# The row loads and sums of the second block's first gate, moved from one output projection to the gated unit and the branch projections after it

## What is computed

```
mod = silu(c) @ w_mod + b_mod                 # 6 x 2048 values, second block
sh1, sc1, g1, sh2, sc2, g2 = split(mod, 6)
...
x = rms_norm(x, final_g)                      # end of the first block
h = rms_norm(x, norm1_g) * (1 + sc1) + sh1
q, k, v, u, gates = split(h @ w_in)           # attention, state-space branch, 2 branch gates
y_ssm = y * sigmoid(y @ w_glu + b_glu)        # the gated unit
merged = sigmoid(gate_a) * (y_attn @ w_attn_br) + sigmoid(gate_s) * (y_ssm @ w_ssm_br)
x = x + g1 * (merged @ w_out)                 # g1 is first needed here
```

## Time and profile before

| | |
|---|---|
| time of 3 launches | median 3036.22 us, 3032.48 to 3045.45 |
| the profiled execution itself | 3027.13 us, of it 3025.4 us span (first to last instruction) |
| mean granted TensorE clock | 0.98 |
| PE busy | 2879.7 us, 95% of the span |
| POOL busy | 1828.3 us, 60% |
| DVE busy | 1689.8 us, 56% |
| ACT busy | 1455.1 us, 48% |
| DMA | 620.46 MB, 205 GB/s on average |

### The profile page before, as it was taken

How to read it: one execution, slowest core, us unless ns; L and a number is a source line. 1 busy time by engine, 2 the same in 40 slices (tenths; PEclk the granted TensorE clock), 3 DMA queues, 4 the chain that set the end, 5 groups by cost and what they waited for, 6 DMA issues and landing times.

```text
span 3025.4 us, 49352 instructions
## 1 busy us (share of the span) xinstructions
PE 2879.7 (95%) x18353; PEld 2486.3 (82%) x18353; DVE 1689.8 (56%) x2879; ACT 1455.1 (48%) x2231; POOL 1828.3 (60%) x756
## 2 busy tenths in 40 slices
PE   7799999999889989999997999999999999999999
PEld 5688886777768888878877888899987888888888
DVE  2477972899533668247669999673324444442000
ACT  3222223556422432248645777675445555555443
POOL 1244443333233565445575677677887888888998
PEclk9999999999999999999998999999999999999999
DMA  9877322555676695233593444444555666765665
GB/s 397 320 264 274 137 97 97 184 193 202 256 271 244 249 396 230 97 105 112 183 348 130 151 154 152 147 147 159 186 191 173 239 238 223 245 215 193 206 208 187
DMA packets 148917, 620.46 MB, mean 205 GB/s; under 512 B 16512, under 2 KB 17840, under 8 KB 129840
## 3 DMA queue, kind: packets, MB, share of 16 engines
q1 hardware_dynamic: 147632, 613.44, 57.0%
q10 hardware_dynamic: 1152, 5.24, 0.5%
HBM read 616.49 MB, written 2.12 MB: 204 GB/s over the span
## 4 chain that ended last, share of the span: by engine, by line
issue 46%; POOL 29%; PE 23%; POOLq 1%; DVE 0%; DVEq 0%
POOL w_low L690 29%; PE bank L725 16%; PE bank L726 8%; POOLq L685 0%; POOLq L689 0%; POOLq L690 0%; DVE region L1866 0%; DVE region L1869 0%; DVEq L1866 0%; POOLq L2675 0%
## 5 line engine op out<-in xcount | busy, mean ns | idle before, releaser
L690 POOL TENSOR_TENSOR w_low<-raw,w_high 128x1024 fp32r<-128x1024 f32 x752 | 1828.1, 2448 | 1186.5 <-ACT w_high L1224 1182.6
L1224 ACT ACTIVATE w_high<-raw 128x1024 fp32r<-128x1024 f32 x752 | 792.9, 1057 | 836.6 <-PE bank L738 410.2
L736 PE MATMUL bank<-h,w_high 128*128 128x256 f32 (+1 forms) x2816 | 951.8, 338 | 18.4 <-POOL w_low L690 15.2
L738 PE MATMUL bank<-h,w_low 128*128 128x256 f32 (+1 forms) x2816 | 935.6, 332 | 0.0
L737 PE MATMUL bank<-h,w_high 128*128 128x256 f32 (+1 forms) x2816 | 935.6, 332 | 0.0
L736 PEld LDWEIGHTS bank<-h,w_high 128*128 128x128 f32 x2816 | 537.7, 191 | 98.9 <-issue 28.6
L725 PE MATMUL bank<-h,w_high 128*128 128x512 f32 x1664 | 584.9, 397 | 9.6 <-POOL w_low L690 4.8
L738 PEld LDWEIGHTS bank<-h,w_low 128*128 128x128 f32 x2816 | 537.4, 191 | 51.0
L737 PEld LDWEIGHTS bank<-h,w_high 128*128 128x128 f32 x2816 | 538.0, 191 | 49.8 <-issue 0.7
L726 PE MATMUL bank<-h,w_low 128*128 128x256 f32 x1664 | 464.3, 279 | 0.0
L725 PEld LDWEIGHTS bank<-h,w_high 128*128 128x128 f32 x1664 | 314.9, 189 | 85.3 <-POOL w_low L690 6.1
(11 more groups left out here) (258 smaller groups left out, 3484.9 us busy)
## 6 DMA issues: line engine op xcount, KB each, us to landing
raw<-in_w_in SPq DMA_DIRECT2D x344, 512.0 KB, 3.7
raw<-in_w_up SPq DMA_DIRECT2D x176, 512.0 KB, 3.8
region<-in_w_rows SPq DMA_DIRECT2D x55, 1024.0 KB, 7.7
raw<-in_w_out SPq DMA_DIRECT2D x96, 512.0 KB, 6.0
raw<-in_w_down SPq DMA_DIRECT2D x96, 512.0 KB, 3.6
region<-in_w_mods SPq DMA_DIRECT2D x44, 1024.0 KB, 7.9
row_extra<-in_w_half_rows SPq DMA_DIRECT2D x86, 512.0 KB, 4.4
row_extra<-in_w_rows SPq DMA_DIRECT2D x41, 1024.0 KB, 7.6
```

Of the source, the lines that this page charges most:

```text
L690: nc.gpsimd.tensor_tensor(WL[s][:, part], RAW[s][:, part], WH[s][:, part], ALU.subtract) \
L736: nc.tensor.matmul(bank[:, 0:n], WH[slot][:, w], h, start=first and j == 0, stop=False)
L738: end = nc.tensor.matmul(bank[:, 0:n], WL[slot][:, w], h, start=False, stop=last and j == len(blocks) - 1)
L1224: return nc.scalar.activation(out, in_, func, **kw)
```

## The change

The stage "out1" becomes a stage "mid". The row loads keep their number and content. Two of the three buffers change: instead of two places of region2 they are `MODW[:, 0]` and `MODW[:, 1]`, which overlap the normalised input of `w_in2`; so row load 1 waits until `w_in2` has been multiplied (`2 * U_GLU`). SP issues them ahead of the units of `w_abr` (row loads 0 to 3 ahead of unit 0, then 4, 5, 6, 7 and 8, 9, 10, 11) and of the first three of `w_sbr` (12 and 13, 14 and 15, 16 and 17). DVE sums 0 to 3 behind the last attention head, ahead of the gated unit's products; then, behind every second tile of `w_abr`: 4, 5, 6, 7 and 8, 9, 10, 11, 12 and 13; and behind tiles 1, 3, 5 and 7 of `w_sbr`: 14, 15, 16, 17. DVE's loop over the tiles of `w_abr` and SP's loops over `w_out1`, `w_abr` and `w_sbr` are written out or become generic accordingly.

```
-    ROW_OUT1 = [ROW_EXTRA[:], *r2(0, 4096)]
+    ROW_MID = [ROW_EXTRA[:], MODW[:, 0, :], MODW[:, 1, :]]
+    mid_rows = lambda r: 4 + 5 * r // 4
...
-        def row_out1(e):
-
+        def row_mid(e):
+
+            if e == 1:
+                sp.wait_ge(halves_done, 2 * U_GLU)
...
-            if name == "w_out1":
-                two(0)
-                two(1)
-                row_out1(0)
-                sp.wait_ge(sem("at_y"), 12)
-                row_out1(1)
-                row_out1(2)
-                for t in range(4, 16):
-                    for e in range(t - 1, t + 3 if t == 15 else t):
-                        row_out1(e)
+            if name in ("w_abr", "w_sbr"):
+                first = [mid_rows(t) for t in range(8)] if name == "w_abr" else [min(18, 14 + 2 * t) for t in range(8)]
+                asked = 0 if name == "w_abr" else mid_rows(7)
+                for t in range(8):
+                    for e in range(asked, first[t]):
+                        row_mid(e)
+                    asked = first[t]
                     one(t)
                 return
...
-            else:
-                for e in range(3):
-                    rows_out1(e)
...
-                elif n < 15:
-                    rows_out1(3 + n)
...
         attended_low(7)
+        for e in range(4):
+            rows_mid(e)
...
-        with dve.Fori(0, 4) as i:
-            for s in range(4):
-                n = 4 * i + s
-                dve.wait_ge(halves_done, 2 * U_ABR + n + 1)
-                mul(tile(GATE_A, n), L[s][:, 0:T], tile(GATE_A, n)).then_inc(bank_free[s], 1)
+        for n in range(KT):
+            dve.wait_ge(halves_done, 2 * U_ABR + n + 1)
+            mul(GATE_A[:, n, :], L[n % 4][:, 0:T], GATE_A[:, n, :]).then_inc(bank_free[n % 4], 1)
+            for e in range(mid_rows(n // 2), mid_rows(n // 2 + 1)) if n % 2 else ():
+                rows_mid(e)
...
             if n >= 4:
                 merged_low(n - 4)
+            if n % 2 and n < 8:
+                rows_mid(14 + n // 2)
```

More of the change, by code:

```diff
@@ L341, in build @@
     ROW_IN1 = [ROW_EXTRA[:], *r2(4096, 6144)]
-    ROW_OUT1 = [ROW_EXTRA[:], *r2(0, 4096)]
+    ROW_MID = [ROW_EXTRA[:], MODW[:, 0, :], MODW[:, 1, :]]
     ROW_UP = [ROW_EXTRA[:]]
-    ROW_STAGES = {"in0": (ROW_IN0, 34), "att0": (ROW_ATT0, 64), "out0": (ROW_OUT0, 34), "in1": (ROW_IN1, 33), "out1": (ROW_OUT1, 18), "up": (ROW_UP, 18)}
+    ROW_STAGES = {"in0": (ROW_IN0, 34), "att0": (ROW_ATT0, 64), "out0": (ROW_OUT0, 34), "in1": (ROW_IN1, 33), "mid": (ROW_MID, 18), "up": (ROW_UP, 18)}
     ROW_FIRST, ROW_LANDED = {}, {}
@@ L537, in row_in1 @@
                 row_load("in1", e, dram["w_rows"][32 + e - 1])
-        def row_out1(e):
+        def row_mid(e):
+            if e == 1:
+                sp.wait_ge(halves_done, 2 * U_GLU)
             if e % 9 == 0:
-                row_cond("out1", e, slice(2, 3), e // 9)
+                row_cond("mid", e, slice(2, 3), e // 9)
             else:
-                row_load("out1", e, dram["w_rows"][64 + 8 * (e // 9) + e % 9 - 1])
+                row_load("mid", e, dram["w_rows"][64 + 8 * (e // 9) + e % 9 - 1])
         def row_up(e):
@@ L2068, in rows_in1, with rows_mid @@
                 row_bias(ROW_ALL["in1"], 96, 32, 2, 3).then_inc(sem("row_out"), 1)
-        def rows_out1(e):
+        def rows_mid(e):
             half, unit = e // 9, e % 9 - 1
             if unit < 0:
-                row_vector("out1", e, 5, HALF)
+                row_vector("mid", e, 5, HALF)
                 return
-            place = row_landed("out1", e)
+            place = row_landed("mid", e)
             for r in range(2):
@@ L2082, in rows_out1 @@
             if e == 17:
-                row_bias(ROW_ALL["out1"], 128, 16, 2, 3, 0).then_inc(sem("row_out"), 1)
+                row_bias(ROW_ALL["mid"], 128, 16, 2, 3, 0).then_inc(sem("row_out"), 1)
         def rows_up(e):
```

## The result

In 20 runs of each the kernel after took 3052.55 us in the median (3038.94 to 3068.03), the kernel before 3039.11 (3027.3 to 3050.65). The ratio is 1.0047, with a 95% interval of 1.0031 to 1.0063: 14 us more, between 9 and 19. The forecast was 8.3 us more and 3044.5. So the sign and the class (within 0.5%) came out, and the cost was put too low.

What follows compares the result with a forecast made beforehand. PE was taken to bound the kernel, busy for 95% of the span. A gain of 7.2 us and a cost of 15.5 gave +8.3 on the 3036.2 us median, so 3044.5 us, range 3029 to 3056.

Steps and rivals of the forecast that it cites:

- the tail: End of the last output projection: the last residual no longer waits for DVE's bias, a gain of 0.6 us.
- The stall of 3.7 us and the slow clock of 2.9: Last output projection, unit 15: PE's wait for POOL's `w_low` and the half clock behind it both go, gaining 3.7 and 2.9.
- my upper bound: Last output projection: at most 7.5 + 2.9 + 0.6 = 11 us gained, if row loads cause every idle spell there.
- The chain behind a sum: Both branches, tiles numbered 0 to 31: 13.8 us from a tile's end to the tile hanging on it, 10.65 from row-load issue.
- the 8.0 us of tile 18: State-space branch, tiles 18 and 19: row load 15 waits for 12, summed behind tile 15; 13.8 against 5.76, stall 8.0 us.
- tile 20 to be covered by the slow clock: State-space branch: the 2.2 us stall there is hidden while PE runs slowly, so only the clock's 2.9 us counts.
- I charge that once: State-space branch: slow clock costs 2.9 us, counted only behind the 8.0 us stall ahead of tile 18.
- hidden: Gated unit: DVE's some 8 us for row loads 0 to 3 cost nothing, as DVE has 0.42 us of work in 23.
- delay DVE but by themselves not PE: Both branches: a tile's bank is wanted again only 11.5 us later, so DVE's row sums alone do not stall PE.
- The full queue: Rival, both branches: three chains each 3.3 us longer behind other transfers, time 3060, halfway 3052; chance 0.16.
- The deeper cover: Rival, both branches: no chain from a row load's wait reaches PE, so the time is 3029.0; chance 0.08.
- the lost gain: Rival, last output projection: another wait replaces the one at unit 15, only the cost is left, 3051.7; chance 0.06.

Runs made afterwards that it cites:

- the reordered kernel before: Kernel before, with the output projection's last three row loads issued behind the weights of unit 15; ratio 0.9996, and 0.9983 on another chip.
- the repeat: The kernel after, unchanged, run again for a second profile; ratio 1.0074 to the kernel before.
- weights first: Kernel after, with each unit's weights issued ahead of the row loads that stood before them; ratio 1.0029 to the kernel before.
- four buffers: Kernel after, with a fourth row-load buffer, so a row load waits for the sum four before instead of three; ratio 1.002 to the kernel before.
- the bank: Kernel after, with DVE's product, sum and low half in the state-space branch working in the tile's PSUM bank; ratio 1.0046 to the kernel before.
- the sums alone: Kernel after without row loads 3 to 17; DVE still makes all 18 sums from what lies in the buffers; ratio 1.0002 to the kernel before.
- loads alone: Kernel after with all 18 row loads but no sums; a row load waits for the landing of the one three before; ratio 1.0031 to the kernel before.
- the kernel without rows: Kernel after with all 18 row loads and their sums left out; ratio 0.9984 to the kernel before.
- all three: Kernel after with a fourth row-load buffer, weights issued ahead of row loads, and DVE's state-space operations in the PSUM bank; ratio 0.9991 to the kernel before.

## Why the prediction was right or wrong

**What came out, and by what luck.** The median lies inside the range of 3029 to 3056, near its upper end. The 24.2 us of the profiled stages on top of 3036.2 would be 3060, outside it. Of the terms of the cost, 12.6 us of stalls were found as 12.1 with errors that cancel; the stalls at tiles 4 and 28 and most of the slow clock stood in no term.

**The gain: two terms right, the tail wrong.** The stall of 3.7 us and the slow clock of 2.9 behind it went: 99.6 to 93.0 us is just their sum, 6.6. For the tail I counted 0.6, and DVE's last residual did move up. PE's last product, DVE's last residual and PE's next product after stand at

```profile
1583.52 0.28 PE L726 MATMUL bank<-h,w_low 128*128 128x256 f32 x1
```
```profile
1583.84 0.48 DVE L1866 SCALAR_TENSOR_TENSOR region<-bank,mod_sb,region 128x256 f32<-128x256 f32 x1 [3.16 <-PE bank L726]
```
```profile
1587.18 1.86 PE L816 MATMUL bank<-region,const_sb 128*128 128x512 f32 x2 [3.38 <-DVE region L1801]
```

The residual follows 0.3 us behind the product instead of the 1.0 of the earlier trace rows, but PE's next product comes 3.7 us behind the last in both kernels. So the tail gave nothing, and up to the next weights 5.9 us were won of 7.2. Of the 7.5 us idle in my upper bound 2.6 lie behind the last product and belong to no stall of the projection. I had also written off DVE's 43 us, as lying beside products. With the stall taken away by a new order alone they lie on the path, as the two runs of the reordered kernel before show: the gain needs the sums to leave as well.

**The chain behind a sum: right for tiles 8, 18 and 20, too short for tile 16.** I had 13.8 us from the end of a tile to the tile that hangs on it. Tile 15's last product starts at 2144.20, and tile 18 starts at 2157.53: 13.3. SP and ACT of the kernel after on that chain, and then on the one of tile 20:

```profile
2147.25 0.33 SPq L509 DMA_DIRECT2D row_extra<-in_w_rows  x1
2147.62 0.91 SPq L464 DMA_DIRECT2D raw<-in_w_sbr  x2
2149.53 10.87 SPq L509 DMA_DIRECT2D mod_weights<-in_w_rows  x2
```
```profile
2153.99 1.06 ACT L1224 ACTIVATE w_high<-raw 128x1024 fp32r<-128x1024 f32 x1 [7.96 <-DMA raw<-in_w_sbr]
...
2166.40 1.06 ACT L1224 ACTIVATE w_high<-raw 128x1024 fp32r<-128x1024 f32 x1 [10.10 <-DMA raw<-in_w_sbr]
```

From row load 15 at 2147.25 to tile 18 are 10.3 us, where I took 10.65 from a single instance. The second of the two row loads in the third line is row load 17: it goes out as that entry ends, 2160.4, and ACT has the weights behind it 6 us later. By the fit that the Trainium skill gives for DMAs issued by GpSimd (DMA: Bandwidth & Descriptors, Anatomy of one DMA) I had estimated 5.6 us for the transfers, which SP issues here; from 2147.25 to 2153.99 it is 6.7, nearer the rows' 7.1.

For tile 16 SP and ACT read

```profile
2135.55 0.91 SPq L464 DMA_DIRECT2D raw<-in_w_sbr  x2
```
```profile
2143.68 1.06 ACT L1224 ACTIVATE w_high<-raw 128x1024 fp32r<-128x1024 f32 x1 [6.49 <-DMA raw<-in_w_sbr]
```

Row load 13 goes out right ahead, at 2135.17, and tile 16 starts at 2147.24: 12.1 us instead of 10.65, in the repeat 11.5. The queue, which I had taken as drained, wasn't: row load 12 had gone out at 2129.09, and the DMA was busy for 0.92 to 1.00 of its time from 2133 to 2143.

**The sum over the chains: wrong in two ways that partly cancel.** First, I counted the 8.0 us of tile 18 from an end of tile 15 that nothing follows, and 2.3 for tile 16 on top, though tile 16's stall lies inside that chain. By the same working it should have been 2.3 and 5.7, and then tile 20, at 21.7 against 11.5 + 5.7, would have had 4.5 and not 2.2. Measured from the end of tile 15 to the start of tile 18: 13.3 instead of 5.8, so 7.6 lost for both tiles with the clock's 1.7 among them, against my 10.3 without it. Second, I held tile 20 to be covered by the slow clock. It wasn't: its chain hangs on the start of tile 16, and 21.7 us were forecast for it, 22.7 measured. Its stall of 4.93 us is the largest of this profile; in the repeat, where tile 18 had lost 5.51, it was 0.92. At tile 8 I had 2.3 and it was 0.36; tile 4 had lost 4.1 already. All stalls of tiles 8 to 20 together come to 12.1 us against my 12.6: this term was right as a sum and wrong in its parts.

**The clock: the step that failed most, "I charge that once".** I tied it to the longest stall, 8.0 us. There was no stall of 8, but five of 2.41 to 4.93, each followed by a stretch near 1.2 GHz: some 10 us instead of 2.9. The 3.7 us of the earlier trace rows were the only case that I had read, and I took it for typical of long stalls instead of asking what the short ones (2.3) would do. The trace of before has others: in the 3 us behind the idle spells of 5.23 us (up to 1644.02) and 6.83 us (up to 1101.64) the granted clock was 0.50, behind 1.51 and 2.20 us (up to 1140.52 and 1905.58) 1.00.

**Tile 4: not seen.** I called row loads 0 to 3 hidden in the gated unit because DVE was idle there. But the DMA went from 0.47 to 0.90 of its time, ACT waited for weights (1.37 us at 2092.93), so its work on the gated unit came later, and everything behind it. DVE and ACT of the kernel after:

```profile
2094.85 6.19 DVE L1795 TENSOR_TENSOR region<-region 128x512 f32<-128x512 f32 x4 [6.88 <-ACT region L1224]
```
```profile
2099.87 1.84 ACT L1224 ACTIVATE y_ssm_high<-region 128x512 fp32r<-128x512 f32 x3 [2.18 <-DVE region L1795]
2101.61 1.99 ACT L1224 ACTIVATE w_high<-raw 128x1024 fp32r<-128x1024 f32 x2
```

The copy of tile 4's weights starts at 2101.61, 33.1 us after the first product of the gated unit; before it was 29.6 after it, with some 1.5 us to spare at the end of POOL's subtraction. Of the 3.5 us, 2.0 are the later start of DVE's four products (26.3 us after the first product of the gated unit, 24.3 before) and 1.5 their length, 6.19 us instead of 4.72. 2.41 us of stall and 1.7 of clock followed. The kernels with the weights first have no stall there, those with four buffers alone or the bank alone have 1.7 and 1.4. So the place of a row load in the queue matters here too. Neither the sums alone nor the loads alone make the stall. With the loads alone the four products take 5.94 us but start at 24.3 as before, and the copy comes 30.8 after the first product, inside the 1.5 us to spare; row load 3, which otherwise waits for the first row sum, goes out without that wait there.

**DVE's durations: taken as fixed.** That the sums "delay DVE but by themselves not PE" holds for the middle, as the run with the sums alone shows; behind it PE waited 4.10 us for DVE in that run, and most of DVE's sums of two tiles were longer than I took them for. With the stalls it doesn't hold in the middle either. From tile 20 on POOL catches up, and DVE after reads

```profile
2180.12 2.19 DVE L1801 TENSOR_TENSOR region<-region 128x256 f32<-128x256 f32 x1
2182.24 2.62 DVE L1798 TENSOR_TENSOR merged<-region,merged 128x256 fp32r<-128x256 f32 x1
2184.78 1.21 DVE L1996 SCALAR_TENSOR_TENSOR mod_weights<-mod_weights,bank 128x1024 f32<-128x1024 f32 x1
```

with row sums in between, until PE waits 4.74 us for a bank at tile 28: with the clock 7 us that no step of mine had. One operation held up in the same way (2.52 us at 2155.24) stands ahead of the sum of row load 14, and so is also in the chain of tile 20.

**The rivals.** The full queue, whose halfway price of 3052 is nearest to the median, has a share, but a small one: its mark was to be chains longer than 10.65, and only that of tile 16 was clearly so, by 1.4 us, against 3.3 on each of three. Those of tiles 8, 18 and 20 were 10.3 and shorter. It is the next bound, though. Once the order is loosened the DMA is at 0.93, and about 5 us of stalls for weights stay. The deeper cover and the lost gain are refuted by the rows above.

**What stays open.** The stages of the profiled execution give 24 us, the ratio 14 (9 to 19), the repeat's ratio 22 (14 to 31) with 19.5 from its stages. The profiled execution of before was 12 us shorter than the median of its 20 runs, that of after 2.7 longer, and no trace shows where the other executions spend it; the stretch between the next weights and the gated unit, in which nothing differs, took 473.1 to 477.2 us in the thirteen profiles. The stalls stand at the same tiles in both profiles, but whether one is 1.70 or 2.76 us differs, and with it whether slow clock follows (1.00 behind the 1.70, 0.50 behind the 2.76). That executions differ in this is likely and wasn't measured.

## What to carry to other kernels

Ask of a stall first whether it is the amount of work or its place in a queue, and measure what its end is worth up to the first product of the next stage: here a new order of three transfers took the stall away, and PE waited as much longer for DVE behind the stage. Moving all eighteen won 5.9 us and cost three (by the ratio) to five times (by the profile) as much. When a sum has several stalls, lay them on one time axis, each chain from the event it hangs on, and charge the slow clock to each, the short ones too. An engine that is paced by the bound one leaves gaps that others live on, so once it is late and runs without gaps, or once the others come at another time, their durations from the old trace no longer hold.

## What the runs showed of the hardware

- VectorE operations of 128x256 with both inputs in SBUF took 0.42 to 0.50 us where they started in the gaps of POOL's subtractions. Where they started inside a subtraction they took up to 2.6 us: with the sums alone 1.35 to 2.57, one of them ending 0.28 us behind the subtraction, and 2.2 to 2.6 beside subtractions of 2.4 to 2.5 us without a gap. With one input in PSUM they took 0.42 to 0.43 throughout. The Trainium skill has this rule (SBUF — State Buffer, SBUF: two separate sides): GpSimd and a VectorE operation with two SBUF inputs exclude each other for the whole instruction. The rows agree. A copy of 128x16 from SBUF to SBUF, with a single input, took 2.33 and 2.19 us there as well (loads alone), 0.66 and 0.18 in the kernel without rows.
- What followed a stall: behind 1.46 (loads alone), 1.59 (all three), 1.70 (the repeat) and 2.23 us (weights first) the granted clock of the next 3 us was 1.00; behind 2.09 (four buffers) 0.62; behind 2.33 (all three) 0.54; behind 2.37 (the bank) 0.63; behind 2.41 in the two profiles of the kernel after 0.59 and 0.54; behind 2.76 and 2.79 0.50; behind 3.19 (four buffers) 0.70; behind 4.7 and more 0.50. So stalls of 2.09 and 2.23 us went either way, and the length of the stall alone doesn't decide it. A stretch cost 1.7 to 2.4 us.
